# Expert chunks of a mixture of experts: ScalarE's Silu table load moved to the chunk's head, and the copy of the result shared with VectorE

## The chip, the cores and the metric

The kernel runs on one core of a Trainium2 chip, in one launch. The metric is the device time of that launch in microseconds (us). The kernel before has a median of 2042.09 us over 3 runs (2041.75 to 2046.13). About 0.2%, some 4 us, is what a measurement of this kernel can tell from no change.

## What is computed

Two layers with shared router weights. Each layer has modulated norms, a mixer (windowed attention beside a gated DeltaNet) and a grouped mixture of experts. The change lies in the experts alone. What they compute, cut from the reference:

```python
D_MODEL, D_FF, N_EXPERTS, DEPTH = 1024, 512, 16, 2      # 128 + 512 tokens, 2 experts each
xs = t[tok].astype(w_gate.dtype)                        # tokens sorted by expert
hid = jax.nn.silu(lax.ragged_dot(xs, w_gate, sizes)) * lax.ragged_dot(xs, w_up, sizes)
y = lax.ragged_dot(hid, w_down, sizes)
y = y * gate.reshape(-1)[order][:, None].astype(y.dtype)
return jnp.zeros((B * L, D), y.dtype).at[tok].add(y).reshape(B, L, D)
```

## The kernel before, in words

The function `expert_phase` runs once per layer. The tokens of an expert are taken in chunks of up to 128; an expert has at least one chunk, and 37 chunks run in the two layers. Only the last chunk of an expert prepares the weights of the next expert (`last and not final` in the code). So there are three kinds of step from a chunk to the next: last to last (24 of them with both ends inside the stretch looked at here), last to not-last (4) and not-last to last (4).

Products are made in three parts, because TensorE's operands are rounded: a weight piece of 128 x 2048 is split into `w_hi` (a rounded copy, ScalarE, `split` at L2061) and `w_lo` (what is left of it, a subtraction). There are six pieces per expert: 0 and 1 of the gate matrix, 2 and 3 of up, 4 and 5 of down. VectorE makes `w_lo` of pieces 0 to 4 (L2121), GpSimd that of piece 5 (L1952). The gathered tokens are turned by TensorE (L1973) and split in the same way into `x_hi` (ScalarE, L2058) and `x_lo` (VectorE, L2116), and so are the turned hidden values (L2096, L2148). The raw pieces of the next expert are loaded by SyncE's queue, each as soon as the `w_lo` before it in its place is made.

Every engine has its own hand-written order (`chunk(e, k, last, final)` in each of the five blocks), with semaphores between them:

- TensorE (L2018 to L2052): second half of the gate product, turn of the next chunk's tokens, the whole up product, then `gate_head`, the first half of the gate product of the next chunk, with the two turns of the hidden values in it, and last the down product into the PSUM banks 5 and 6 (L2043, L2044, L2049). `gate_head` waits for `x_lo` of the next chunk and for `w_lo` of piece 0.
- ScalarE (L2070 to L2105): `next_hi(0)`, a one-element Silu (L2081, tile `warm`) that brings in Silu's table, the Silu of the gate (L2084), `x_hi` and the pieces 1 to 4 in turn, then the copy of the finished result `y` out of PSUM (L2101, 128 x 1024), `next_hi(5)`, and the DMA of `y` to DRAM (L2105), which ScalarE's own queue issues after a wait for the copy. Behind this the queue runs the loop's branches and register loads, and the next chunk begins.
- VectorE (L2123 to L2152): `w_lo` of piece 0, the first half of `x_lo`, the two halves of `hid`, piece 1, the hidden low parts, the second half of `x_lo`, pieces 2, 3 and 4.
- GpSimd (L1949 to L1961): the gather of tokens two chunks ahead, and `w_lo` of piece 5.

Of the kernel before, what the change touches and what calls it, by code (L numbers as in the profile page):

```python
# [14 lines left out]
ACT = mybir.ActivationFunctionType  # L15
# [1843 lines left out]
def expert_phase(nc, l, A, G, R):  # L1859
# [11 lines left out]
    with ExitStack() as ctx:  # L1871
        ph = Phase(nc, ctx, "expert", l)
# [12 lines left out]
        y = ph.sb("y", [P, D])  # L1885
        cur = ph.sb("cur_idx", [P, 1], I32)
        warm = ph.sb("warm", [P, 1])
        raw_in = [ph.sem(f"raw_in{j}") for j in range(PIECES)]
        picked, g_half, g_p, u_half, u_p, xt_p, ht_p, d_half, y_p, w_hi_done, w_lo_done = (
            ph.sem(n) for n in "picked g_half g_p u_half u_p xt_p ht_p d_half y_p w_hi_done w_lo_done".split())  # L1890
        w_lo_last = ph.sem("w_lo_last")
        sg_done, hid_done, x_hi_done, x_lo_done, h_hi_done, h_lo_done, y_done, y_out, passed = (
            ph.sem(n) for n in "sg_done hid_done x_hi_done x_lo_done h_hi_done h_lo_done y_done y_out passed".split())
        gathered = ph.dma_sem(G.soft["gathered"])
# [9 lines left out]
        def hid_turned(m):  # L1904
            return G.ps[:, 4 + 3 * m, 0:HQ * P]
# [16 lines left out]
        with nc.Block() as block:  # L1922
# [45 lines left out]
            @block.tensor  # L1968
            def _(pe):
                def turn(k):  # L1970
                    pe.wait_ge(gathered, k * 16 + 16)
                    for n in range(KD):
                        tr = pe.transpose(turned[:, n * P:(n + 1) * P], xg[:, n:D:KD], G.c("ident"))  # L1973
                    tr.then_inc(xt_p, 1)

                def hid_turn(k, m):
                    pe.wait_ge(hid_done, k * 2 + (m + 2))
                    for n in range(HQ):
                        q = m * HQ + n
                        tr = pe.transpose(hid_turned(m)[:, n * P:(n + 1) * P], hid[:, q:FF:KF], G.c("ident"))  # L1980
                    tr.then_inc(ht_p, 1)

                def product(bank, q, j):

                    w, at = slice(q % 4 * FF, q % 4 * FF + 512), slice(q * P, (q + 1) * P)
                    pe.matmul(bank, x_hi[:, at], w_hi[:, j, w], start=(q == 0), stop=False)  # L1986
                    pe.matmul(bank, x_hi[:, at], w_lo[:, j, w], start=False, stop=False)  # L1987
                    return pe.matmul(bank, x_lo[:, at], w_hi[:, j, w], start=False, stop=(q == KD - 1))  # L1988

                def gate(q):  # L1990
                    return product(G.ps[:, 0, :], q, q // 4)

                def up(q):
                    return product(G.ps[:, 1, :], q, 2 + q // 4)

                def gate_head(e, k, between):

                    pe.wait_ge(x_lo_done, k * 2 + 1)
                    pe.wait_ge(w_lo_done, e * LP + 1)
                    for q in range(4):  # L2000
                        mm = gate(q)
                        if q in between:
                            between[q]()
                    mm.then_inc(g_half, 1)

                for s in (u_p, xt_p, ht_p, y_p):
                    pe.sem_inc(s, 1)
                turn(0)
                gate_head(0, 0, {})

                def chunk(e, k, last, final):
                    pe.wait_ge(x_lo_done, k * 2 + 2)
                    pe.wait_ge(w_lo_done, e * LP + 2)
                    for q in range(4, KD):
                        mm = gate(q)
                    mm.then_inc(g_p, 1)
                    if not (last and final):
                        turn(k + 1)  # L2018
                    pe.wait_ge(hid_done, k * 2 + 1)
                    for q in range(KD):  # L2020
                        if q % 4 == 0:
                            pe.wait_ge(w_lo_done, e * LP + (3 + q // 4))
                        mm = up(q)
                        if q % 4 == 3:
                            mm.then_inc((u_half, u_p)[q // 4], 1)
                    if last and final:
                        hid_turn(k, 0)
                        hid_turn(k, 1)
                    else:
                        pe.wait_ge(sg_done, k + 1)  # L2030
                        gate_head(e + 1 if last else e, k + 1, {1: lambda: hid_turn(k, 0), 2: lambda: hid_turn(k, 1)})
                    pe.wait_ge(y_done, k + 1)
                    for q in range(KF):
                        j, at = 4 + q // 2, slice(q * P, (q + 1) * P)
                        if q == 0:
                            pe.wait_ge(w_lo_done, e * LP + LP)
                        if q == 2:
                            pe.wait_ge(w_lo_last, e + 1)
                        if q % HQ == 0:
                            pe.wait_ge(h_hi_done, k * 2 + (q // HQ + 1))  # L2040
                        for h in range(2):
                            w = slice(q % 2 * D + h * 512, q % 2 * D + (h + 1) * 512)
                            pe.matmul(G.ps[:, 5 + h, :], h_hi[:, at], w_hi[:, j, w], start=(q == 0), stop=False)  # L2043
                            pe.matmul(G.ps[:, 5 + h, :], h_hi[:, at], w_lo[:, j, w], start=False, stop=False)  # L2044
                        if q % HQ == 0:
                            pe.wait_ge(h_lo_done, k * 2 + (q // HQ + 1))
                        for h in range(2):
                            w = slice(q % 2 * D + h * 512, q % 2 * D + (h + 1) * 512)
                            mm = pe.matmul(G.ps[:, 5 + h, :], h_lo[:, at], w_hi[:, j, w], start=False, stop=(q == KF - 1))  # L2049
                        if q % 2:  # L2050
                            mm.then_inc((d_half, y_p)[q // 2], 1)

                for_experts(pe, chunk)

            @block.scalar
            def _(act):
                def take(m):
                    act.activation(x_hi[:, x_half(m)], turned[:, x_half(m)], ACT.Copy).then_inc(x_hi_done, 1)  # L2058

                def split(j):  # L2060
                    act.activation(w_hi[:, j, :], raw[:, j, :], ACT.Copy).then_inc(w_hi_done, 1)  # L2061
# [10 lines left out]
                def chunk(e, k, last, final):  # L2072
                    def next_hi(j):

                        if last and not final:
                            act.wait_ge(raw_in[j], e * 16 + 16)
                            act.wait_ge((g_half, g_p, u_half, u_p, d_half, y_p)[j], k + (1, 1, 1, 2, 1, 2)[j])
                            split(j)

                    next_hi(0)  # L2080
                    act.activation(warm[:, :], G.eps[:, :], ACT.Silu)  # L2081
                    act.wait_ge(g_p, k + 1)
                    act.wait_ge(hid_done, k * 2 + 1)
                    act.activation(sg[:, :], G.ps[:, 0, :], ACT.Silu).then_inc(sg_done, 1)  # L2084
                    if not (last and final):
                        act.wait_ge(xt_p, k + 3)
                        act.wait_ge(u_half, k + 1)
                        take(0)
                    next_hi(1)
                    if not (last and final):  # L2090
                        act.wait_ge(u_p, k + 2)
                        take(1)
                    act.wait_ge(y_p, k + 1)
                    for m in range(2):
                        act.wait_ge(ht_p, k * 2 + (m + 2))
                        act.activation(h_hi[:, m * HQ * P:(m + 1) * HQ * P], hid_turned(m), ACT.Copy).then_inc(h_hi_done, 1)  # L2096
                        next_hi(2 + m)
                    next_hi(4)
                    act.wait_ge(y_p, k + 2)
                    act.wait_ge(y_out, k * 16 + 16)  # L2100
                    act.activation(y[:, :], G.ps[:, 5:7, :].rearrange("p b n -> p (b n)"), ACT.Copy).then_inc(y_done, 1)  # L2101
                    next_hi(5)
                    act.wait_ge(y_done, k + 2)
                    dst = A.y_table.rearrange("(c p) n -> c p n", p=P)[bass.ds(k, 1)].rearrange("a p n -> p (a n)")
                    act.dma_start(dst, y[:, :]).then_inc(y_out, 16)  # L2105

# [6 lines left out]
            def _(dve):  # L2113
# [6 lines left out]
                    dve.wait_ge(w_hi_done, e * PIECES + (j + 1))  # L2120
                    dve.tensor_tensor(w_lo[:, j, :], raw[:, j, :], w_hi[:, j, :].bitcast(F32), ALU.subtract).then_inc(w_lo_done, 1)  # L2121

                dve.sem_inc(hid_done, 1)  # L2123
                split(0, 0)
                for m in range(2):
                    take(0, m)
# [3 lines left out]
                def chunk(e, k, last, final):  # L2130
                    def next_lo(j):
                        if last and not final:
                            split(e + 1, j)
# [16 lines left out]
                            take(k + 1, 1)  # L2150
                    for j in range(2, LP):
                        next_lo(j)  # L2152

                for_experts(dve, chunk)
        ph.close()
# [164 lines left out]
```

## Time and profile before

| what | value |
|---|---|
| median of 3 runs | 2042.09 us |
| time of the profiled execution | 2047.7 us |
| its span, first to last instruction | 2045.9 us |
| TensorE busy (share of the span) | 1757.2 us (86%) |
| VectorE busy | 1219.8 us (60%) |
| ScalarE busy | 1022.2 us (50%) |
| GpSimd busy | 403.9 us (20%) |

The busy times are unions of the instructions' intervals on an engine. TensorE's (PE) are pipelined, so that 86% is not 86% of its peak. In the rows below DVE is VectorE, ACT is ScalarE, POOL is GpSimd, PEld is TensorE's weight load, and a q behind an engine's name is its queue (its sequencer), which waits, branches and issues DMAs. The expert phases lie at about 663 to 1040 us and 1650 to 2013 us of the span.

### The profile page before, as it was taken

The page shows a single profiled execution, that of the slowest core. Times are in us where ns is not written, and L with a number is a line of the kernel's source. Part 1 is how long each engine was busy: PE and PEld are TensorE (multiplying, and loading weights), DVE is VectorE, ACT ScalarE, POOL GpSimd, SP SyncE. Part 2 cuts the span into 40 slices and gives each one's busy share as a digit, 9 for nine tenths or more (in the row PEclk, how much of TensorE's full clock was granted, in tenths as well). Part 3 has the DMA queues.
Part 4 walks back from the last instruction along what each step waited for, and adds up shares of the span by engine and source line. Part 5 has one row for each costly group of instructions (what it writes and reads, how often), then busy time and mean ns, then how long its engine had stood idle before and what let it go on. Part 6 is the DMA issues. An engine that isn't in the chain of part 4 may idle for free. (4 is left out here: it accounts for less than half of the span.)

```text
span 2045.9 us, 39615 instructions
## 1 busy us (share of the span) xinstructions
PE 1757.2 (86%) x15349; PEld 1444.1 (71%) x15350; DVE 1219.8 (60%) x1815; ACT 1022.2 (50%) x1564; POOL 403.9 (20%) x293
## 2 busy tenths in 40 slices
PE   3998988999896899999949998899989959999992
PEld 0898677788653778778738886788875547777872
DVE  1388254566545875875554873556663477777563
ACT  2244522333422886886644454233332258888661
POOL 0000022212100342342230001212220024334221
PEclk7999998999897899999969999999998979999996
DMA  7221093331114898997563111342003279999854
GB/s 317 72 83 45 18 376 127 125 126 54 63 65 165 333 376 309 338 377 269 215 224 113 42 44 55 125 152 69 2 2 116 83 296 369 366 391 370 321 195 175
DMA packets 113580, 376.62 MB, mean 184 GB/s; under 512 B 15178, under 2 KB 35938, under 8 KB 87846
## 3 DMA queue, kind: packets, MB, share of 16 engines
q1 hardware_dynamic: 84782, 303.86, 40.3%
q10 hardware_dynamic: 20168, 39.89, 5.1%
q0 software_dynamic: 8496, 30.94, 4.1%
q8 instruction: 103, 1.69, 0.3%
q14 instruction: 31, 0.25, 0.0%
HBM read 332.87 MB, written 41.78 MB: 183 GB/s over the span
## 5 line engine op out<-in xcount | busy, mean ns | idle before, releaser
L2121 DVE TENSOR_TENSOR expert_w_lo<-shared,expert_w_hi 128x2048 fp32r<-128x2048 f32 x160 | 389.6, 2468 | 166.5 <-ACT expert_w_hi L2061 166.4
L2061 ACT ACTIVATE expert_w_hi<-shared 128x2048 fp32r<-128x2048 f32 x192 | 366.8, 1915 | 46.5 <-PEq L143 40.0
L1986 PE MATMUL ps<-expert_w_hi,expert_x_hi 128*128 128x512 f32 x592 | 245.8, 415 | 49.3 <-DVE expert_x_lo L2116 49.3
L1988 PE MATMUL ps<-expert_w_hi,expert_x_lo 128*128 128x512 f32 x592 | 233.8, 395 | 0.0
L1987 PE MATMUL ps<-expert_w_lo,expert_x_hi 128*128 128x512 f32 x592 | 233.7, 395 | 0.0
L1952 POOL TENSOR_TENSOR expert_w_lo<-shared,expert_w_hi 128x2048 fp32r<-128x2048 f32 x32 | 150.8, 4712 | 364.9 <-ACT expert_w_hi L2061 364.9
L1986 PEld LDWEIGHTS ps<-expert_w_hi,expert_x_hi 128*128 128x128 f32 x592 | 113.6, 192 | 81.2 <-DVE expert_w_lo L2121 51.2
L1127 POOL TENSOR_TENSOR mixer_NTb<-mixer_Bt,consts_sb 128x256 f32<-128x256 f32 x120 | 88.4, 760 | 283.3 <-DVE mixer_Bt L1402 220.1
L1988 PEld LDWEIGHTS ps<-expert_w_hi,expert_x_lo 128*128 128x128 f32 x592 | 112.6, 190 | 24.3
L1987 PEld LDWEIGHTS ps<-expert_w_lo,expert_x_hi 128*128 128x128 f32 x592 | 113.2, 191 | 18.7
L2043 PE MATMUL ps<-expert_w_hi,expert_hid_hi 128*128 128x512 f32 x296 | 115.8, 391 | 0.5 <-ACT expert_hid_hi L2096 0.5
L2044 PE MATMUL ps<-expert_w_lo,expert_hid_hi 128*128 128x512 f32 x296 | 115.3, 390 | 0.0
L1420 DVE TENSOR_TENSOR mixer_X<-mixer_X,ps 128x256 f32<-128x256 f32 x100 | 42.1, 421 | 109.1 <-PE ps L1216 107.2
L624 PE MATMUL ps<-projection_hT_hi,kvrows_r 128*128 128x256 f32 (+1 forms) x384 | 89.9, 315 | 9.6 <-DVE shared_r L531 9.6
L1339 ACT ACTIVATE mixer_T<-ps 128x256 f32<-128x256 f32 x100 | 38.4, 384 | 119.1 <-PE ps L1216 115.3
L2049 PE MATMUL ps<-expert_w_hi,expert_hid_lo 128*128 128x512 f32 x296 | 91.1, 389 | 0.0
L588 PE MATMUL ps<-shared_r,projection_hT_hi 128*128 128x512 f32 (+1 forms) x240 | 89.2, 372 | 0.0
L628 PE MATMUL ps<-projection_hT_hi,shared_r 128*128 128x256 f32 (+1 forms) x384 | 88.1, 311 | 0.0
L801 DVE SCALAR_TENSOR_TENSOR shared<-shared,projection_cwT 128x644 f32<-128x644 f32 x96 | 85.2, 888 | 2.5
L959 POOL MEMSET qkvT<- 128x512 f32 (+1 forms) x2 | 0.8, 418 | 393.6 <-POOLq L143 393.6
L624 PEld LDWEIGHTS ps<-projection_hT_hi,kvrows_r 128*128 128x128 f32 x384 | 70.0, 191 | 10.8 <-DVE shared_r L531 10.7
L1573 PE MATMUL ps<-shared,qkvT 128*128 128x512 f32 x160 | 76.0, 620 | 0.0
(372 smaller groups left out, 3856.5 us busy)
## 6 DMA issues: line engine op xcount, KB each, us to landing
shared<-in_w_up SPq DMA_DIRECT2D x64, 1024.0 KB, 7.5
shared<-in_w_down SPq DMA_DIRECT2D x64, 1024.0 KB, 8.1
shared<-in_w_gate SPq DMA_DIRECT2D x64, 1024.0 KB, 7.3
qkv<-in_w_ada SPq DMA_DIRECT2D x20, 1280.0 KB, 6.3
shared<-in_w_in SPq DMA_DIRECT2D x10, 2048.0 KB, 8.4
y_table<-expert_y ACTq DMA_DIRECT2D x37, 512.0 KB
qkvT<-in_w_ada SPq DMA_DIRECT2D x20, 768.0 KB, 8.6
y_table<-zero ACTq DMA_DIRECT2D x1, 12800.0 KB, 50.9
```

The lines of the kernel that those rows point to most:

```text
L588: pe.matmul(out, hi, w_lo, start=False, stop=False)
L624: pe.matmul(out, w_hi[:, k, :], h_hi[:, k, t * P:until * P], start=(k == 0), stop=False)
L1127: return pool.tensor_tensor(NTb[:, slot, d], Bt[:, d], row(G.c(f"level{level}_{d}"), DH), ALU.mult)
L1952: pool.tensor_tensor(w_lo[:, LP, :], raw[:, LP, :], w_hi[:, LP, :].bitcast(F32), ALU.subtract).then_inc(w_lo_last, 1)
L1986: pe.matmul(bank, x_hi[:, at], w_hi[:, j, w], start=(q == 0), stop=False)
L1987: pe.matmul(bank, x_hi[:, at], w_lo[:, j, w], start=False, stop=False)
L1988: return pe.matmul(bank, x_lo[:, at], w_hi[:, j, w], start=False, stop=(q == KD - 1))
L2043: pe.matmul(G.ps[:, 5 + h, :], h_hi[:, at], w_hi[:, j, w], start=(q == 0), stop=False)
L2044: pe.matmul(G.ps[:, 5 + h, :], h_hi[:, at], w_lo[:, j, w], start=False, stop=False)
L2049: mm = pe.matmul(G.ps[:, 5 + h, :], h_lo[:, at], w_hi[:, j, w], start=False, stop=(q == KF - 1))
L2061: act.activation(w_hi[:, j, :], raw[:, j, :], ACT.Copy).then_inc(w_hi_done, 1)
L2121: dve.tensor_tensor(w_lo[:, j, :], raw[:, j, :], w_hi[:, j, :].bitcast(F32), ALU.subtract).then_inc(w_lo_done, 1)
```

## The change

Three edits. ScalarE's one-element Silu moves from behind `next_hi(0)` to ahead of it. ScalarE copies only bank 5 of the result (128 x 512); bank 6 is copied by VectorE, at the end of its chunk, behind the `w_lo` of pieces 2 to 4. A new semaphore `y_low` says that VectorE's half is done; TensorE waits for it ahead of the next down product, and ScalarE ahead of the DMA of `y`.

```diff
-        w_lo_last = ph.sem("w_lo_last")
+        w_lo_last, y_low = ph.sem("w_lo_last"), ph.sem("y_low")
...
                     pe.wait_ge(y_done, k + 1)
+                    pe.wait_ge(y_low, k + 1)
                     for q in range(KF):
...
+                    act.activation(warm[:, :], G.eps[:, :], ACT.Silu)
                     next_hi(0)
-                    act.activation(warm[:, :], G.eps[:, :], ACT.Silu)
                     act.wait_ge(g_p, k + 1)
...
                     act.wait_ge(y_p, k + 2)
                     act.wait_ge(y_out, k * 16 + 16)
-                    act.activation(y[:, :], G.ps[:, 5:7, :].rearrange("p b n -> p (b n)"), ACT.Copy).then_inc(y_done, 1)
+                    act.activation(y[:, 0:512], G.ps[:, 5, :], ACT.Copy).then_inc(y_done, 1)
                     next_hi(5)
                     act.wait_ge(y_done, k + 2)
+                    act.wait_ge(y_low, k + 2)
                     dst = A.y_table.rearrange("(c p) n -> c p n", p=P)[bass.ds(k, 1)].rearrange("a p n -> p (a n)")
                     act.dma_start(dst, y[:, :]).then_inc(y_out, 16)
...
-                dve.sem_inc(hid_done, 1)
+                for s in (hid_done, y_low):
+                    dve.sem_inc(s, 1)
...
                     for j in range(2, LP):
                         next_lo(j)
+                    dve.wait_ge(y_p, k + 2)
+                    dve.wait_ge(y_out, k * 16 + 16)
+                    dve.tensor_copy(y[:, 512:1024], G.ps[:, 6, :]).then_inc(y_low, 1)
```

**The head of a chunk on ScalarE**, for the last chunk of an expert. Before:

```order
L2076 ISA
L2077 REGISTER_ALU
L2061 ACT_TABLE_LOAD
L2061 ACTIVATE expert_w_hi<-shared 128x2048
L2081 ACT_TABLE_LOAD
L2081 ACTIVATE expert_warm<-eps 128x1
L2083 ISA
L2084 ACTIVATE expert_sg<-ps 128x512
```

And in the changed kernel (line numbers from L2030 on are one higher, and more further down):

```order
L2081 ACT_TABLE_LOAD
L2081 ACTIVATE expert_warm<-eps 128x1
L2077 ISA
L2078 REGISTER_ALU
L2062 ACTIVATE expert_w_hi<-shared 128x2048
L2084 ISA
L2085 ACTIVATE expert_sg<-ps 128x512
```

One of the two table loads is gone: the copy of piece 0 (`w_hi`) needs none when Silu's table has been loaded ahead of it. The other now stands ahead of the register steps that wait for piece 0.

**The end of a chunk on VectorE**, where the copy of bank 6 comes in, in the changed kernel (before, the branch followed the third subtraction):

```order
L2123 TENSOR_TENSOR expert_w_lo<-shared,expert_w_hi 128x2048
L2122 REGISTER_ALU
L2123 TENSOR_TENSOR expert_w_lo<-shared,expert_w_hi 128x2048
L2157 ISA
L2158 COPY expert_y<-ps 128x512
L1918 REGISTER_ALU
L1918 COMPARE_AND_BRANCH
```

The last two rows are the loop's own steps: the copy is the last work of the chunk.

**The end of a chunk on ScalarE**, in the changed kernel; the shape of the copy and what ScalarE's queue waits for at L2107 are all that differs from before:

```order
L2102 ACTIVATE expert_y<-ps 128x512
L2062 ACTIVATE expert_w_hi<-shared 128x2048
L2107 ISA
L2107 DMA y_table<-expert_y 128x1024
L1918 REGISTER_ALU
L1918 COMPARE_AND_BRANCH
```

The branch and the register loads of the loop stand behind the DMA and its waits in the same queue.

## Rows read from the trace of the kernel before

**Rows 1.** The page: busy us, share of the span, instructions, by engine.
```profile
PE 1757.2 (86%) x15349; PEld 1444.1 (71%) x15350; DVE 1219.8 (60%) x1815; ACT 1022.2 (50%) x1564; POOL 403.9 (20%) x293
```
**Rows 2.** Busy time by stretch: PE, PEld, DVE, ACT, POOL, then clock, DMA share, GB/s.
```profile
695.77:1036.35 340.58, 320.65 (x1492) 263.65 (x1490) 216.31 (x177) 256.84 (x241) 111.02 (x49) 1.00 0.85 319
869.09:888.62 19.53, 18.08 (x86) 14.82 (x85) 14.88 (x12) 16.97 (x15) 7.80 (x3) 1.00 0.98 374
793.28:811.05 17.77, 17.77 (x86) 14.91 (x85) 5.16 (x8) 6.77 (x9) 5.72 (x3) 1.00 0.76 287
...
686.35:689.70 3.35, 3.35 (x11) 2.54 (x11) 2.54 (x3) 2.13 (x3) 0.00 (x0) 0.50 0.97 391
```
**Rows 3.** Waits by total: us, times, longest; 695:1036, then 1686:2010.
```profile
PE ps L1986 <- DVE expert_x_lo L2116: 18.9, 14, 1.5
...
PE ps L1986 <- DVE expert_x_lo L2116: 19.9, 14, 1.5
```
**Rows 4.** Timeline, ScalarE: start us, us, instruction, [idle before and what ended it].
```profile
869.09 1.03 ACT L2101 ACTIVATE expert_y<-ps 128x1024 f32<-128x1024 f32 x1 [0.81 <-PE ps L2049]
870.01 1.91 ACT L2061 ACTIVATE expert_w_hi<-shared 128x2048 fp32r<-128x2048 f32 x1
870.27 0.34 ACTq L2105 DMA_DIRECT2D y_table<-expert_y  x1
872.09 1.28 ACT L2061 ACT_TABLE_LOAD   x1 [0.17 <-issue]
873.38 1.92 ACT L2061 ACTIVATE expert_w_hi<-shared 128x2048 fp32r<-128x2048 f32 x1
875.32 1.28 ACT L2081 ACT_TABLE_LOAD   x1
876.62 0.20 ACT L2081 ACTIVATE expert_warm<-eps 128x1 f32<-128x1 f32 x1
876.72 0.58 ACT L2084 ACTIVATE expert_sg<-ps 128x512 f32<-128x512 f32 x1
877.20 0.59 ACT L2058 ACTIVATE expert_x_hi<-ps 128x512 fp32r<-128x512 f32 x1
```
**Rows 5.** Timeline, VectorE, the same step from chunk to chunk.
```profile
866.96 4.49 DVE L2121 TENSOR_TENSOR expert_w_lo<-shared,expert_w_hi 128x2048 fp32r<-128x2048 f32 x2
875.34 3.43 DVE L2121 TENSOR_TENSOR expert_w_lo<-shared,expert_w_hi 128x2048 fp32r<-128x2048 f32 x1 [3.89 <-ACT expert_w_hi L2061]
878.69 0.68 DVE L2116 TENSOR_TENSOR expert_x_lo<-ps,expert_x_hi 128x512 fp32r<-128x512 f32 x1
```
**Rows 6.** Timeline, GpSimd, the same step.
```profile
872.00 4.62 POOL L1952 TENSOR_TENSOR expert_w_lo<-shared,expert_w_hi 128x2048 fp32r<-128x2048 f32 x1 [10.90 <-ACT expert_w_hi L2061]
```
**Rows 7.** Timeline, TensorE: the first matmul of `gate_head` in this step.
```profile
879.52 0.49 PE L1986 MATMUL ps<-expert_w_hi,expert_x_hi 128*128 128x512 f32 x1 [1.45 <-DVE expert_x_lo L2116]
```
**Rows 8.** Timeline, ScalarE and TensorE, a step of the second layer.
```profile
1783.87 1.03 ACT L2101 ACTIVATE expert_y<-ps 128x1024 f32<-128x1024 f32 x1 [0.82 <-PE ps L2049]
...
1787.05 1.28 ACT L2061 ACT_TABLE_LOAD   x1 [0.35 <-issue]
...
1794.29 0.49 PE L1986 MATMUL ps<-expert_w_hi,expert_x_hi 128*128 128x512 f32 x1 [1.45 <-DVE expert_x_lo L2116]
```
**Rows 9.** Timeline, a step from a not-last to a last chunk: ScalarE, TensorE.
```profile
811.05 1.03 ACT L2101 ACTIVATE expert_y<-ps 128x1024 f32<-128x1024 f32 x1 [5.85 <-PE ps L2049]
...
814.45 1.28 ACT L2061 ACT_TABLE_LOAD   x1 [2.37 <-issue]
...
821.02 0.49 PE L1986 MATMUL ps<-expert_w_hi,expert_x_hi 128*128 128x512 f32 x1 [1.00 <-DVE expert_x_lo L2116]
```
**Rows 10.** Lines of the whole kernel, VectorE: another PSUM copy of that shape.
```profile
L926 DVE COPY kvrows<-ps 128x512 f32<-128x512 f32 x10 | 6.5, 687 | 6.2 <-PE ps L659 5.9
```
**Rows 11.** Timeline of the first chunk of layer one: TensorE, VectorE.
```profile
685.15 0.49 PE L1986 MATMUL ps<-expert_w_hi,expert_x_hi 128*128 128x512 f32 x1 [2.68 <-DVE expert_x_lo L2116]
...
690.40 6.88 DVE L2121 TENSOR_TENSOR expert_w_lo<-shared,expert_w_hi 128x2048 fp32r<-128x2048 f32 x3
```

## The prediction

> **What bounds the kernel now.** I read the page first, then busy time by stretch, then the waits, then the timeline of one step. The page [rows 1] shows TensorE at 86% and everything else far below, so time is lost or won where TensorE stands still. In the first expert phase it does so for 340.58 - 320.65 = 19.9 us [rows 2], and the waits name one cause for 18.9 us of it: the first matmul of `gate_head` waits for VectorE's `x_lo`, 14 times there and 14 times in the second layer [rows 3]. A last-to-last step takes 19.53 us with 18.08 us of TensorE [rows 2]; the 1.45 us between them is that wait [rows 7].
>
> So the question is what makes `x_lo` late. Count from Y, the start of ScalarE's result copy (869.09). ScalarE: copy to Y+1.03, high part of piece 5 to Y+2.83, table load at Y+3.00, high part of piece 0 from Y+4.29 to Y+6.21 [rows 4]. VectorE then subtracts piece 0 from Y+6.25 and needs 3.43 us, where the two subtractions before it took 4.49 us together, so about 2.28 each [rows 5]. The reader should see GpSimd beside it: its own subtraction runs from Y+2.91 to Y+7.53 [rows 6], and VectorE ends 2.15 us behind that, as if it had only begun when GpSimd ended. So TensorE is held by two things in turn: ScalarE's chain sets when VectorE may begin, GpSimd's instruction when it really does. `x_lo` follows at once (0.68 us), TensorE restarts at Y+10.43.
>
> **The Silu at the chunk's head.** Before, ScalarE loads a table, splits piece 0, loads Silu's table, and makes the one-element Silu (0.20 us) [rows 4]. Now the first load is Silu's and the second is gone, in 30 last chunks. ScalarE still has one load of 1.28 us ahead of piece 0, plus the small Silu, which delays it by 0.11 (876.62 to the next start at 876.72, and 0.01 of gap). What is saved, 1.28 us, lies behind piece 0, where in a last-to-last step nobody waits: `x_hi` ends at Y+8.70 and VectorE reaches `x_lo` only at Y+9.60 [rows 4, 5]. In the four not-last-to-last steps GpSimd is not in the way, and the path is ScalarE's: table load at Y+3.40, and TensorE idles 1.00 us [rows 9]. There `x_hi` is 1.28 us earlier, and VectorE's piece 0 is next. With the result copy 0.38 us shorter (below): load at Y+2.90, piece 0 from Y+4.30 to Y+6.22, VectorE to Y+8.54, `x_lo` to Y+9.14, TensorE at Y+9.29; it was at Y+9.97. That is 0.68 us for each, **-2.7 us** for four.
>
> A row against a rule: the load of 1.28 us starts 0.02 us behind the work before it and the next instruction starts 0.02 us behind it [rows 4]. The Trainium skill, ScalarE: Activation LUTs, What ACT_TABLE_LOAD costs, adds a drain of about 1.38 us to every switch; by it those four steps would win their whole 1.00 us, -4.0 us instead of -2.7. The trace shows no drain on this chip, so I keep the rows.
>
> **The result copy.** ScalarE's copy of 512 columns costs about what the Silu of that size does, 0.58 us [rows 4], so 0.45 less than 1.03. VectorE's half is priced by a copy of the same shape out of PSUM, 0.69 us [rows 10]. But VectorE comes to it only behind its third subtraction, which ends at 866.96 + 4.49 = 871.45, Y+2.36 [rows 5]. With the 0.08 us by which its instructions overlap, the copy runs from Y+2.28 to **Y+2.97**.
>
> **The new wait.** ScalarE's queue waits for that before it issues the DMA. Before, it had only its own copy to wait for (Y+1.03): DMA issue at 870.27, then the loop's branches and register loads, and the table load at 872.09, 1.97 us behind the copy's end. Those 1.97 us ran under the split of piece 5, which ended at Y+2.83; only 0.17 us showed as idle [rows 4]. That split was the cover, and it is gone: queued behind the wait are the DMA, the loop, the table load and piece 0. The order rows put the load ahead of two register steps; no row prices them, the bounds are 0 and the 0.17 us of idle, and I take 0.12 off, so 1.85 us. The load then starts at Y+4.82 and ends at Y+6.10, piece 0 runs from Y+6.22 to Y+8.13, VectorE's subtraction from Y+8.15. GpSimd, started 0.45 us earlier, has ended by Y+7.1 (by Y+7.6 if VectorE's copy held it off), so the subtraction takes its plain 2.28 us, to Y+10.43. `x_lo` overlaps it by 0.08 and ends at Y+11.03, TensorE restarts 0.15 later at **Y+11.18** instead of Y+10.43: +0.75 us. In the second layer the same branches take longer, 2.15 us from the copy's end to the load (1784.90 to 1787.05), for a restart at Y+10.42 [rows 8]; there it is Y+11.36, +0.94 us.
>
> Of the 24 steps, the first of each layer differs: VectorE ends at Y+1.51 there (690.40 + 6.88 against a Y of 695.77) [rows 11], so its copy ends at Y+2.12 and the step is about even in layer one, and some 0.5 us longer in layer two. The sum: 10 x 0.75 + 12 x 0.94 + 0.5 = **+19.3 us**.
>
> **Parts that cost nothing.** The four last-to-not-last steps have TensorE busy for all of 17.77 us [rows 2]; their Silu comes 2 us later, to about Y+6.9, and `x_lo` would be there at Y+8.1, against a TensorE free at Y+8.98; if that 0.9 us were used up they would pay too. TensorE's wait for `y_low` stands ahead of the next down product, far behind the copy, and the new copy's wait for the DMA of the chunk before (`y_out`) is for one issued a whole step earlier. VectorE's 0.69 us lie in its 3.89 us of idle [rows 5]. At the end of each layer the final result leaves 0.38 us earlier, **-0.8 us**.
>
> **The clock.** TensorE's gap grows from 1.45 to about 2.2 us in layer one and 2.4 in layer two. At 1.45 the granted clock stayed 1.00 (2.4 GHz) over the whole phase [rows 2]. After the gap of 2.68 us in the first chunk [rows 11] it read 0.50 (1.2 GHz) from 686.35 to 689.70 [rows 2]. The new gap lies between these two. What such a drop costs: from the restart to the next Y took 695.77 - 685.15 = 10.62 us there and 888.62 - 879.52 = 9.10 in a plain step, 1.52 us more on TensorE; but VectorE's third subtraction ended only 0.69 us later behind the restart (12.13 against 11.44), and VectorE is what the next step hangs on. So a drop costs 0.7 us, and the gap behind it is short again (about 1.35 us). The bounds are no drop at all and one after every second gap at the full 1.52, 0 to 18 us. The gap of 2.2 to 2.4 us is nearer to 2.68 than to 1.45, and none follows directly on a drop; I take a third of the gaps, 8 x 0.7 = **+5.6 us**.
>
> **Sum.** 19.3 - 2.7 - 0.8 + 5.6 = +21.4 us. Against the profiled execution's 2047.7 us that makes 2069.1. That execution lies 5.6 us above the median of the runs, so the median should be 2042.1 + 21.4 = **2063.5 us**.
>
> **Rivals.**
>
> *The shorter copy frees GpSimd, and it is faster.* By the rows GpSimd's subtraction is what VectorE really waits for; it begins when piece 5 is split, which is 0.45 us earlier now. If ScalarE's queue lost nothing at the new wait, each of the 24 steps would be 0.44 us shorter: -10.6 - 2.7 - 0.8 = -14 us, 2028 us. The Trainium skill, SBUF — State Buffer, Who interferes with whom, says that a VectorE instruction with two SBUF inputs and a GpSimd one that reads SBUF exclude each other whole; VectorE's end 2.15 us behind GpSimd's agrees, and by that rule alone this rival is the outcome. It decides if VectorE's copy is done by about Y+2.2, since the rest of the path takes 8.2 us; the rows put it at Y+2.97. A DMA share of 0.98 in a step [rows 2] speaks against it too: the weight loads leave little room for a shorter step, and a longer one relieves them. 8 in 100.
>
> *The two effects meet.* If the loop's steps cost less once nothing runs beside them, or the copy waits less, the restart stays within 0.15 us of now and the 24 steps add under 4 us: 2039 to 2046 us. Against it: it needs 0.6 us off a chain whose rows hardly vary. 6 in 100.
>
> *The clock falls after most gaps.* If VectorE falls behind as much as TensorE after each drop, and 14 gaps have one, it is 14 x 1.52 = 21 in place of 5.6: 2042.1 + 15.8 + 21 = 2079 us. For it, the distance to 2.68; against it, the first chunk's 0.69. 8 in 100.
>
> That the change would not do what it says is excluded for the table load: the order rows show it gone.
>
> **How the numbers follow.** The forecast has 78 in 100. Its own range goes from no drops and 1.8 us of loop in both layers (19.3 becomes 16; +12.5) to 8 more drops at full cost (+34). I give 2051 to 2077, which leaves out the faster and the even case and most of the third rival. A measurement can tell 0.2%, 4 us: faster 0.08, same 0.06, slower 0.86.
>
> **What would show it.** Right: ScalarE's table loads at L2061 gone (30 of them, 38 us of ScalarE), the one load per last chunk at about Y+4.8 with some 2 us of idle ahead of it instead of 0.17, VectorE's subtraction of piece 0 at 2.28 us, TensorE's gap at 2.2 to 2.4 us, and the step at 20.3 to 20.5 us. Wrong: a step under 19.5 us, VectorE's copy ending before Y+2.2, or the load starting earlier than 1.8 us behind VectorE's copy. The number of stretches at 1.2 GHz inside the expert phases settles the clock term.

## The result, and the profile after

The changed kernel takes 2066.18 us (median of 4 runs, 2064.75 to 2068.91) against 2043.69 us of the kernel before on the same chips (4 runs, 2041.75 to 2046.13). The ratio is 1.0111 with a 95% interval of 1.0093 to 1.0129: slower by 22.5 us, where 21.4 had been forecast. The profiled execution took 2064.75 us, with a span of 2063.0 us.

The page gives the busy times of the changed kernel, which answer to [rows 1]:

```profile
PE 1761.8 (85%) x15349; PEld 1445.9 (70%) x15350; DVE 1217.0 (59%) x1852; ACT 963.9 (47%) x1534; POOL 358.9 (17%) x293
```

Every helper engine works less than before, ScalarE by 58 us, and the kernel is slower. VectorE has 25.3 us of copies more and is still no busier, since its subtraction of piece 0 no longer lasts 3.43 us. GpSimd's 45 us less lie in its 37 index copies of 128x1 (L1944), which take 372 ns each instead of 1715. The groups of lines say what happened (count | busy us, mean ns of one | idle before, and what ended it):

```profile
L2081 ACT ACT_TABLE_LOAD x34 | 43.6, 1283 | 78.3 <-issue 78.2
L2158 DVE COPY expert_y<-ps 128x512 f32<-128x512 f32 x37 | 25.3, 684 | 37.4 <-PE ps L2050 37.4
L2102 ACT ACTIVATE expert_y<-ps 128x512 f32<-128x512 f32 x37 | 22.1, 598 | 65.2 <-PE ps L2050 65.2
```

The 30 table loads ahead of piece 0 are gone (38.5 us of ScalarE). The 34 that stay have 78.2 us of idle ahead of them that ended with "issue": ScalarE stood ready, and its queue had not yet come to the instruction.

A last-to-last step of layer one, Y = 875.05. ScalarE's timeline (compare [rows 4]):

```profile
875.05 0.60 ACT L2102 ACTIVATE expert_y<-ps 128x512 f32<-128x512 f32 x1 [0.82 <-PE ps L2050]
875.54 1.91 ACT L2062 ACTIVATE expert_w_hi<-shared 128x2048 fp32r<-128x2048 f32 x1
878.20 0.34 ACTq L2107 DMA_DIRECT2D y_table<-expert_y  x1
879.87 1.28 ACT L2081 ACT_TABLE_LOAD   x1 [2.41 <-issue]
881.16 0.20 ACT L2081 ACTIVATE expert_warm<-eps 128x1 f32<-128x1 f32 x1
881.27 1.90 ACT L2062 ACTIVATE expert_w_hi<-shared 128x2048 fp32r<-128x2048 f32 x1
883.08 0.57 ACT L2085 ACTIVATE expert_sg<-ps 128x512 f32<-128x512 f32 x1
```

VectorE's, GpSimd's and TensorE's in the same step (compare [rows 5 to 7]):

```profile
872.90 4.49 DVE L2123 TENSOR_TENSOR expert_w_lo<-shared,expert_w_hi 128x2048 fp32r<-128x2048 f32 x2
877.30 0.68 DVE L2158 COPY expert_y<-ps 128x512 f32<-128x512 f32 x1
883.21 2.29 DVE L2123 TENSOR_TENSOR expert_w_lo<-shared,expert_w_hi 128x2048 fp32r<-128x2048 f32 x1 [5.22 <-ACT expert_w_hi L2062]
...
877.54 4.61 POOL L1952 TENSOR_TENSOR expert_w_lo<-shared,expert_w_hi 128x2048 fp32r<-128x2048 f32 x1 [13.69 <-ACT expert_w_hi L2062]
...
886.25 0.49 PE L1986 MATMUL ps<-expert_w_hi,expert_x_hi 128*128 128x512 f32 x1 [2.22 <-DVE expert_x_lo L2118]
```

Read it as a chain. VectorE's copy ends at 877.98 (Y+2.93). ScalarE's queue issues the DMA at 878.20, not at Y+1.2 as before, and the table load follows at Y+4.82, after 2.41 us of idle that was 0.17. The split of piece 0 starts at Y+6.22, 1.93 us later than before, VectorE subtracts it in its plain 2.29 us because GpSimd ended at 882.15, and TensorE restarts at Y+11.20. In the second layer (compare [rows 8]) the load and the restart stand at Y+5.02 and Y+11.39, with Y = 1855.21:

```profile
1860.23 1.28 ACT L2081 ACT_TABLE_LOAD   x1 [2.61 <-issue]
...
1866.60 0.49 PE L1986 MATMUL ps<-expert_w_hi,expert_x_hi 128*128 128x512 f32 x1 [2.42 <-DVE expert_x_lo L2118]
```

Busy time by stretch (PE, PEld, DVE, ACT, POOL, then clock, DMA share, GB/s): that step, a not-last-to-last one (compare [rows 9]), a step with a stretch of low clock, the step behind it, and the stretch of low clock itself:

```profile
875.05:895.32 20.27, 18.05 (x86) 14.82 (x85) 14.29 (x13) 15.14 (x14) 5.72 (x3) 1.00 0.97 367
...
814.53:832.95 18.42, 18.04 (x86) 14.82 (x85) 12.05 (x11) 13.39 (x13) 1.15 (x2) 1.00 0.57 180
713.04:734.93 21.89, 19.64 (x86) 15.81 (x85) 14.88 (x14) 15.13 (x14) 5.73 (x3) 0.92 0.93 345
734.93:754.74 19.81, 18.05 (x86) 14.82 (x85) 13.84 (x12) 15.15 (x14) 7.56 (x3) 1.00 0.97 362
724.75:728.10 3.35, 3.35 (x11) 2.56 (x10) 2.62 (x4) 0.80 (x2) 0.00 (x0) 0.50 1.01 419
```

Five such stretches at 1.2 GHz lie in the two expert phases behind their first chunks; before there was none. Summed over all steps from one result copy to the next, the changed kernel is 24.9 us longer than before: +27.3 in the 24 last-to-last steps, -2.5 in the four not-last-to-last ones, 0.0 elsewhere. The two profiled spans differ by 17.1 us only; the rest, 7.7 us less, lies outside these steps, 2.3 us ahead of layer one's first result copy and 5.4 us between the layers. The first chunks take 32.3 us in both kernels, and the medians (22.5 us) are the better measure.

### The profile page after: what moved, and what is told of

It is laid out like the page before. It is cut to its first block and busy times, and to the rows that moved or that the text cites. A ratio compares the mean times of both kernels' runs of the same rounds, so it can differ in the third digit from the quotient of the medians.

```text
span 2063.0 us, 39735 instructions
## 1 busy us (share of the span) xinstructions
PE 1761.8 (85%) x15349; PEld 1445.9 (70%) x15350; DVE 1217.0 (59%) x1852; ACT 963.9 (47%) x1534; POOL 358.9 (17%) x293
## 5 line engine op out<-in xcount | busy, mean ns | idle before, releaser
L2123 DVE TENSOR_TENSOR expert_w_lo<-shared,expert_w_hi 128x2048 fp32r<-128x2048 f32 x160 | 365.6, 2318 | 168.8 <-ACT expert_w_hi L2062 168.8
L1988 PEld LDWEIGHTS ps<-expert_w_hi,expert_x_lo 128*128 128x128 f32 x592 | 114.0, 193 | 24.9
L2081 ACT ACT_TABLE_LOAD x34 | 43.6, 1283 | 78.3 <-issue 78.2
```

## The experiments

My theory was that the loss is all in what ScalarE's queue holds behind its wait for VectorE's half: loop, table load and piece 0. The rivals: the moved Silu costs; the shared copy itself costs; GpSimd's subtraction is still what binds. "Plain" below means a step without low clock.

**e1, the Silu alone.** The kernel before with one edit:

```diff
+                    act.activation(warm[:, :], G.eps[:, :], ACT.Silu)
                     next_hi(0)
-                    act.activation(warm[:, :], G.eps[:, :], ACT.Silu)
```

> Only the Silu moves to the chunk's head; ScalarE copies the whole result again and nothing waits for VectorE's half. My theory (the queue's wait for VectorE's copy makes the whole loss): last-to-last steps stay at 19.5 us with TensorE's gap at 1.45 us, because GpSimd's subtraction ends at Y+7.53 as before; the four not-last-to-last steps get some 0.3 us shorter (table load off the path of x_hi, then VectorE's piece 0 binds); in all -1 us against the kernel before. Rival (the moved Silu delays piece 0 and that is what costs): steps of 19.6 us and more, +2.6 us or more, and the half copy alone would then be cheap.

Measured: 2041.69 us, ratio 0.9988 (0.9980 to 0.9997), 2.2 us faster. All 24 last-to-last steps stay at 19.5 us with a gap of 1.45 us; the four others take 18.70 instead of 19.03 to 19.07. The Silu's move is no cost; its gain is small because in the common step GpSimd's instruction covers it.

**e2, the shared copy alone.** The changed kernel with the Silu back behind piece 0.

```diff
-                    act.activation(warm[:, :], G.eps[:, :], ACT.Silu)
                     next_hi(0)
+                    act.activation(warm[:, :], G.eps[:, :], ACT.Silu)
```

> Only the result copy is shared, the Silu stays behind piece 0. My theory: steps of 20.2 us in layer one and 20.5 in layer two as in the changed kernel (the load is now for Copy and starts about 1.9 us behind VectorE's copy), not-last-to-last steps 0.38 us shorter than before (18.67), in all +20 to +25 us against before. Rival (the Silu costs): within 3 us of before.

Measured: 2078.68 us, ratio 1.0162 (1.0142 to 1.0181), 35 us slower: more than I expected, and more than both edits together. Plain steps take 20.6 us in both layers. ScalarE, VectorE and TensorE in one of them (Y = 1889.12):

```profile
1894.10 1.28 ACT L2062 ACT_TABLE_LOAD   x1 [2.58 <-issue]
...
1897.33 1.28 ACT L2082 ACT_TABLE_LOAD   x1
...
1899.21 0.59 ACT L2059 ACTIVATE expert_x_hi<-ps 128x512 fp32r<-128x512 f32 x1
...
1897.34 2.29 DVE L2123 TENSOR_TENSOR expert_w_lo<-shared,expert_w_hi 128x2048 fp32r<-128x2048 f32 x1 [5.27 <-ACT expert_w_hi L2062]
1899.83 0.69 DVE L2118 TENSOR_TENSOR expert_x_lo<-ps,expert_x_hi 128x512 fp32r<-128x512 f32 x1 [0.19 <-ACT expert_x_hi L2059]
...
1900.66 0.49 PE L1986 MATMUL ps<-expert_w_hi,expert_x_hi 128*128 128x512 f32 x1 [2.57 <-DVE expert_x_lo L2118]
```

What I had missed: once GpSimd no longer holds VectorE off, VectorE is done with piece 0 before `x_hi` is there, and the second table load is on the path (the 0.19 us that end with ScalarE's `x_hi`). So beside the shared copy the Silu at the head is worth 0.3 us of each layer-one step, though beside GpSimd's subtraction it was worth nothing. The larger gap (2.58 us) also has ten stretches of low clock behind it instead of five.

**e3, VectorE's copy ahead of its last subtraction.** The changed kernel with its three lines moved up:

```diff
-                    for j in range(2, LP):
+                    for j in range(2, LP - 1):
                         next_lo(j)
                     dve.wait_ge(y_p, k + 2)
                     dve.wait_ge(y_out, k * 16 + 16)
                     dve.tensor_copy(y[:, 512:1024], G.ps[:, 6, :]).then_inc(y_low, 1)
+                    next_lo(LP - 1)
```

> The changed kernel, but VectorE copies its half ahead of the subtraction of piece 4 instead of behind it, so at about Y+0.1 to Y+0.8. My theory: the table load starts at about Y+2.5 behind piece 5; but the subtraction of piece 4 then runs from Y+0.75 to Y+3.0 and keeps GpSimd's subtraction, ready at Y+2.5, from starting until Y+3.0, so GpSimd ends at Y+7.6 and TensorE restarts at about Y+10.45: steps of 19.5 us, no 1.2 GHz stretches behind the first chunk, and with 18.4 us for the not-last-to-last steps -3 us against before. Rival (GpSimd and VectorE don't exclude each other, ScalarE's chain alone counts): restart at about Y+9.0, steps near 18.1 us, -30 us. Rival (GpSimd may start at once): steps of 19.1 us, -13 us.

Measured: 2037.21 us, ratio 0.9968 (0.9957 to 0.9980). The same work in another order is 29 us faster than the changed kernel and 6.6 us faster than the one before. Steps take 19.37 to 19.44 us, and no stretch of low clock lies behind a first chunk. VectorE and GpSimd (Y = 865.07):

```profile
865.14 0.68 DVE L2158 COPY expert_y<-ps 128x512 f32<-128x512 f32 x1
865.75 2.28 DVE L2123 TENSOR_TENSOR expert_w_lo<-shared,expert_w_hi 128x2048 fp32r<-128x2048 f32 x1
871.05 3.62 DVE L2123 TENSOR_TENSOR expert_w_lo<-shared,expert_w_hi 128x2048 fp32r<-128x2048 f32 x1 [3.02 <-ACT expert_w_hi L2062]
...
867.56 4.96 POOL L1952 TENSOR_TENSOR expert_w_lo<-shared,expert_w_hi 128x2048 fp32r<-128x2048 f32 x1 [10.48 <-ACT expert_w_hi L2062]
```

GpSimd was ready at 867.56 but needed 4.96 us instead of 4.62, as VectorE's subtraction ran to 868.03; it ended at 872.52, and VectorE's piece 0, begun at 871.05, ended 2.15 us behind that. The early copy took the wait away, and the old bound came back: the 0.45 us that ScalarE wins shrink to 0.1.

**e4, piece 5 on VectorE, with the kernel before's copy.** e1, and the subtraction of piece 5 moved from GpSimd to the end of VectorE's chunk:

```diff
                         gather(nc.s_assert_within(k + 2, 2, MAXC))
-                        if last:
-                            split_last(e + 1)
...
                     for j in range(2, LP):
                         next_lo(j)
+                    if last and not final:
+                        split_last(e + 1)
```

> e1, and in addition the low part of piece 5 is made by VectorE at its chunk's end instead of by GpSimd. VectorE is idle from Y+2.36 to Y+6.25 and the subtraction needs 2.28 us there once piece 5 is split at Y+2.83. My theory (GpSimd's instruction is what binds the kernel before, by keeping VectorE off): VectorE takes piece 0 at Y+6.3 for 2.28 us, TensorE's gap falls from 1.45 to about 0.4 us, steps of 18.5 us, -24 us against before. Rival (the weight loads bind, DMA share 0.98 in a step): ScalarE waits for raw pieces and steps stay at 19.1 to 19.5 us, -10 to 0 us. Rival (VectorE becomes the bound): steps over 19.5 us, slower.

Measured: 2007.00 us, ratio 0.9823 (0.9806 to 0.9841), 37 us faster, of which 2 are e1's and 35 this move's. VectorE's timeline and the stretch of the step (Y = 855.00):

```profile
857.86 2.29 DVE L2118 TENSOR_TENSOR expert_w_lo<-shared,expert_w_hi 128x2048 fp32r<-128x2048 f32 x1 [0.51 <-ACT expert_w_hi L2054]
861.19 2.29 DVE L2114 TENSOR_TENSOR expert_w_lo<-shared,expert_w_hi 128x2048 fp32r<-128x2048 f32 x1 [1.03 <-ACT expert_w_hi L2054]
...
855.04:873.35 18.31, 18.05 (x86) 14.83 (x85) 16.11 (x13) 15.68 (x15) 2.41 (x2) 1.00 1.02 420
```

VectorE's piece 0 begins where it did before (Y+6.2) and takes 2.29 us instead of 3.43; steps fall to 18.3 (18.5 in layer two) from 19.5. The steps account for 26.7 us, 1.3 of them e1's. A further 7.5 us come from the first chunks, where TensorE waited in the same way (28.5 us to the first result copy instead of 32.3). The weight loads kept up, at 420 GB/s instead of 374.

**e5, ScalarE's queue freed.** The changed kernel, with the DMA of `y` and its two waits in GpSimd's queue, behind its subtraction, and a small first DMA in that queue ahead of the first gather:

```diff
-                    act.wait_ge(y_done, k + 2)
-                    act.wait_ge(y_low, k + 2)
-                    act.dma_start(dst, y[:, :]).then_inc(y_out, 16)
...
+                    pool.wait_ge(y_done, k + 2)
+                    pool.wait_ge(y_low, k + 2)
+                    pool.dma_start(dst, y[:, :]).then_inc(y_out, 16)
```

> The changed kernel, but the DMA of the result and its two waits stand in GpSimd's queue, behind its subtraction of piece 5, instead of in ScalarE's; VectorE's copy stays at the end of its chunk. My theory (the loss is what queues behind the wait on ScalarE): the table load follows piece 5 at about Y+2.5, GpSimd binds again (from Y+2.5 to Y+7.1, which holds VectorE off until then), TensorE restarts at about Y+10.0: steps of 19.1 us, no 1.2 GHz stretch behind the first chunk, -13 us against before. Rival (VectorE's copy itself, or TensorE's new wait, costs): steps stay over 20 us, +20 us.

Measured: 2034.22 us, ratio 0.9954 (0.9935 to 0.9972), 9.5 us faster. VectorE's copy stays as late as in the changed kernel, and it no longer matters. ScalarE, VectorE and GpSimd (Y = 865.79), the step, and a result copy of ScalarE in layer two:

```profile
868.21 1.28 ACT L2086 ACT_TABLE_LOAD   x1
...
868.06 0.68 DVE L2159 COPY expert_y<-ps 128x512 f32<-128x512 f32 x1
871.54 3.50 DVE L2124 TENSOR_TENSOR expert_w_lo<-shared,expert_w_hi 128x2048 fp32r<-128x2048 f32 x1 [2.80 <-ACT expert_w_hi L2068]
...
868.27 4.62 POOL L1953 TENSOR_TENSOR expert_w_lo<-shared,expert_w_hi 128x2048 fp32r<-128x2048 f32 x1 [10.46 <-ACT expert_w_hi L2068]
...
865.77:884.85 19.08, 18.05 (x86) 14.82 (x85) 15.53 (x13) 15.37 (x14) 7.81 (x4) 1.00 0.99 380
...
1758.36 0.60 ACT L2107 ACTIVATE expert_y<-ps 128x512 f32<-128x512 f32 x1 [2.22 <-DMA y_table<-expert_y]
```

This is the rival of the prediction, alive as soon as its condition holds: GpSimd starts 0.43 us earlier than before, VectorE ends 2.15 us behind it, and the step is 0.43 us shorter. I had expected 13 us in all. The steps give 11.3, although one DMA of `y`, issued at 1744.92, landed late and held up ScalarE's copy at 1758.36: that step took 20.5 us, and the next one, with a stretch of 1.2 GHz, 20.7. The first chunks are 3.3 and 3.6 us longer. The first DMA of the new queue is the likely cause: in e10, where it stands behind the first gather, they are 1.3 us longer than in e4 and e7.

**e6, VectorE copies twice.** The changed kernel with the same copy into a spare tile ahead of its own.

```diff
+                    dve.tensor_copy(sg2[:, :], G.ps[:, 6, :])
                     dve.tensor_copy(y[:, 512:1024], G.ps[:, 6, :]).then_inc(y_low, 1)
```

> The changed kernel with VectorE copying the bank twice, the first time into a spare tile: y_low comes 0.6 us later. My theory (each us of y_low's lateness is a us of every last-to-last step): steps of 20.9 us in layer one and 21.1 in layer two, gaps of 2.85 to 3.05 us, 1.2 GHz behind most of the gaps, so at least +14 us against the changed kernel (+36 us against before) and with the clock up to +30 (+52). Rival (VectorE's and ScalarE's spare time cover it): no change against the changed kernel.

Measured: 2101.72 us, ratio 1.0280 (1.0260 to 1.0300): 58 us over the kernel before, 36 over the changed one. The two plain steps of layer one take 20.84 and 20.91 us, 0.6 more for 0.6 us of copy. Most gaps, of 2.0 to 3.3 us, have a stretch of low clock behind them, so the total is over my upper figure.

**e7, the late copy with piece 5 on VectorE.** The changed kernel with e4's second edit.

> The changed kernel with the low part of piece 5 on VectorE, behind its late copy. My theory (in the changed kernel the wait alone sets the step, GpSimd has dropped out): steps stay at 20.3 and 20.5 us, +14 to +24 us against before, although the same move took 1.0 to 1.2 us off every step in e4. Rival (GpSimd still binds): steps of 19.1 to 19.3 us.

Measured: 2061.24 us, ratio 1.0090 (1.0071 to 1.0108). Its plain step:

```profile
751.87:772.16 20.29, 18.04 (x86) 14.82 (x85) 16.52 (x14) 15.13 (x14) 2.42 (x2) 1.00 0.97 359
```

The step is the changed kernel's, 20.29 us. Freeing VectorE of GpSimd, worth 1.2 us a step in e4, is worth nothing behind the wait. The 5 us under the changed kernel come from the first chunks, 28.5 us to the first result copy instead of 32.3 in both layers (7.6 us); the steps take 2.4 us more in sum, with six stretches of low clock instead of five.

**e8, all three that help.** e3 with e4's second edit: Silu at the head, copy ahead of piece 4, piece 5 on VectorE.

> e3 with the low part of piece 5 on VectorE: Silu at the head, VectorE's copy ahead of piece 4, no subtraction on GpSimd. My theory: ScalarE's load at Y+2.65 (2.85 in layer two), VectorE's piece 0 from Y+5.98 (6.17), TensorE's gap 0.05 (0.25) us, steps of 18.1 (18.3) us, 18.4 for the not-last-to-last ones: -6 us against e4, -42 against before. Rival (weight loads bind under 18.3 us a step): no faster than e4. Rival (VectorE late with pieces 4 and 5, busy without a break from Y+0.1 to Y+5.3): piece 0 starts late or TensorE waits in the down product, slower than e4.

Measured: 2003.00 us, ratio 0.9799 (0.9783 to 0.9815). Steps of a layer each:

```profile
837.26:855.42 18.16, 18.05 (x86) 14.82 (x85) 16.66 (x14) 15.29 (x14) 2.42 (x2) 1.00 1.00 392
1730.80:1749.09 18.29, 18.06 (x86) 14.83 (x85) 16.61 (x14) 15.26 (x14) 2.42 (x2) 1.00 1.00 403
```

That is within 0.06 us of the forecast; against e4 the steps' sum is 6.0 us less and the medians differ by 4.0.

**e9, the wait without the shared copy.** ScalarE copies the whole result; VectorE only clears one element per partition at its end.

```diff
-                    act.activation(y[:, 0:512], G.ps[:, 5, :], ACT.Copy).then_inc(y_done, 1)
+                    act.activation(y[:, :], G.ps[:, 5:7, :].rearrange("p b n -> p (b n)"), ACT.Copy).then_inc(y_done, 1)
...
-                    dve.tensor_copy(y[:, 512:1024], G.ps[:, 6, :]).then_inc(y_low, 1)
+                    dve.memset(mark[:, :], 0.0).then_inc(y_low, 1)
```

> The changed kernel with the wait but without the shared copy: ScalarE copies the whole result again, and VectorE only clears one element per partition at the end of its chunk, which y_low then tells of. My theory (the place of the wait costs, the copy behind it only adds its own 0.6 us): y_low comes at about Y+2.4 to Y+2.5, the table load at Y+4.3 in layer one and Y+4.5 in layer two, steps of 19.7 and 19.9 us, so +7 us against before in the 24 steps, and -1 us for the others: about +6. Rival (sharing the copy costs, not the wait): like e1, no slower than before.

Measured: 2056.74 us, ratio 1.0072 (1.0053 to 1.0091), 12.6 us slower where I expected 6. The load stands at Y+4.26 and plain steps take 19.71 us in layer one and 19.91 and 19.95 in layer two (the others there have low clock or follow a step that has it), as forecast. ScalarE (Y = 867.93), and two steps of layer two:

```profile
870.52 0.34 ACTq L2108 DMA_DIRECT2D y_table<-expert_y  x1
872.19 1.28 ACT L2082 ACT_TABLE_LOAD   x1 [1.43 <-issue]
...
1700.02:1721.63 21.61, 19.60 (x86) 15.78 (x85) 14.44 (x14) 15.56 (x15) 7.38 (x3) 0.92 0.95 361
...
1721.63:1741.12 19.49, 18.04 (x86) 14.83 (x85) 13.32 (x12) 15.55 (x15) 7.80 (x3) 1.00 0.96 359
```

The rest is the clock: six steps of layer two have a stretch of 1.2 GHz behind a gap of only 1.86 to 2.01 us. In layer one, with gaps of 1.65 to 1.75 us, there is none.

**e10, the freed queue with piece 5 on VectorE.** e5 with e4's second edit, and the first DMA of the queue behind the first gather.

> e5 with the low part of piece 5 on VectorE (behind its late copy), and the small first DMA of the new queue behind the first gather. My theory: ScalarE's load at Y+2.42 in both layers, VectorE's piece 0 from Y+5.76, TensorE never idle: steps of 18.05 us, 17.76 for the not-last-to-last ones, -5 to -7 us against e8, so about 1997 us. Rival (result DMAs from GpSimd's queue share the DMA engines with the weight loads and land late, as one step of 20.5 us in e5 hints): single long steps, no faster than e8.

Measured: 1997.38 us, ratio 0.9781 (0.9760 to 0.9803), 47 us faster than before and the fastest of all:

```profile
854.50:872.38 17.88, 17.88 (x86) 14.83 (x85) 16.61 (x14) 15.38 (x15) 3.21 (x3) 1.00 1.00 406
```

TensorE is busy without a gap, in steps of 17.85 to 17.91 us (the first of each layer takes 18.05 and 18.06). No step with a late DMA showed here.

| kernel | Silu first | copy of bank 6 | waits for it | piece 5 | plain step, layer 1 / 2 | ratio |
|---|---|---|---|---|---|---|
| before | no | ScalarE | - | GpSimd | 19.5 / 19.5 | 1 |
| e1 | yes | ScalarE | - | GpSimd | 19.5 / 19.5 | 0.9988 |
| e2 | no | VectorE, late | ScalarE | GpSimd | 20.6 / 20.6 | 1.0162 |
| changed | yes | VectorE, late | ScalarE | GpSimd | 20.3 / 20.5 | 1.0111 |
| e7 | yes | VectorE, late | ScalarE | VectorE | 20.3 / 20.5 | 1.0090 |
| e6 | yes | VectorE, late, twice | ScalarE | GpSimd | 20.9 / - | 1.0280 |
| e9 | yes | ScalarE | ScalarE, for a mark | GpSimd | 19.7 / 19.9 | 1.0072 |
| e3 | yes | VectorE, early | ScalarE | GpSimd | 19.4 / 19.4 | 0.9968 |
| e5 | yes | VectorE, late | GpSimd | GpSimd | 19.1 / 19.1 | 0.9954 |
| e4 | yes | ScalarE | - | VectorE | 18.3 / 18.5 | 0.9823 |
| e8 | yes | VectorE, early | ScalarE | VectorE | 18.2 / 18.3 | 0.9799 |
| e10 | yes | VectorE, late | GpSimd | VectorE | 17.9 / 17.9 | 0.9781 |

## Why the prediction was right, point by point

**What bounds the kernel: right.** That TensorE waits for VectorE, which waits for GpSimd's instruction, is shown by e4: VectorE starts piece 0 at the same place, GpSimd's subtraction is gone, and the gap falls from 1.45 to 0.26 us in layer one and to 0.45 to 0.60 in layer two. e3 and e5 show the same 2.15 us from GpSimd's end to VectorE's, wherever GpSimd starts.

**The new wait: right, and the whole cause, with the low clock that follows the longer gaps.** Restart at Y+11.18 and Y+11.36 forecast, Y+11.20 and Y+11.39 measured. The plain steps of layer one cost 0.76 us each (0.75 forecast), those of layer two 0.99 on average (0.94 forecast), and with the first of each layer they come to 19.9 us where the sum said 19.3. e5 shows that it is the queue: with the waits elsewhere the late copy costs nothing. e6 shows the slope, e7 that GpSimd has no part in it, and e9 splits it: the place of the wait alone is worth 0.2 and 0.4 us a step, the copy behind it the other 0.55.

**The Silu at the head: right in this kernel, incomplete as a rule.** -2.7 us was forecast for the four not-last-to-last steps, -2.5 measured, and restarts at Y+9.35 (forecast Y+9.29). That is 0.62 us each, not the 1.00 that the prediction reckoned if there were a drain; nor would that follow from its own path, on which VectorE's piece 0 comes next. "In a last-to-last step nobody waits" was read from the rows of before, where GpSimd still held VectorE off. It fails as soon as that is gone: e2 against the changed kernel shows the second load on the path. The changed kernel was spared this only since both edits came together. No drain behind a table load shows in any run, as in the rows of before: all but four loads of each run have the next instruction 0.01 us behind them.

**The clock: the count and the size were both off, in opposite directions.** The term said 8 x 0.7 = 5.6 us. There were five stretches of low clock, and such a step took 1.5 to 1.6 us more, of which the next step gave back 0.5 once and next to nothing otherwise: 27.3 - 19.9 = 7.4 us. The step of the working that failed is the 0.7 us, taken from one first chunk, and with it the short gap of 1.35 us behind a drop: behind the five it was 1.76 us once and 2.14 to 2.42 three times, and one was followed by a last-to-not-last step, which has no gap to shorten.

In that first chunk the low clock began 1.17 us behind TensorE's restart (686.32 against 685.15). In the changed kernel it began between 0.28 us ahead of the restart and 0.80 us behind it, and the traces show that this place sets the price. The changed kernel, e2, e6, e7 and e9 have 47 such stretches behind a gap ahead of `gate_head`. In the 14 that begin 1.05 us or more behind the restart, VectorE's third subtraction ends at Y+1.5 of the next step, as behind the first chunk, and so the copy behind it comes early. In 10 of the 12 that begin at least 0.1 us ahead of the restart it ends at Y+2.3, as in a plain step; the other two, both in e6, are twice as long. Between these places the end moves steadily from 2.3 to 1.6. Two steps of e2 in a row, the first with low clock from 1.5 us behind the restart, and the stretch of low clock:

```profile
1763.59:1785.79 22.20, 19.62 (x86) 15.94 (x85) 15.43 (x14) 16.53 (x15) 5.72 (x3) 0.92 0.94 353
1785.79:1805.57 19.78, 18.06 (x86) 14.83 (x85) 13.64 (x12) 16.55 (x16) 7.24 (x3) 1.00 0.97 339
1776.66:1780.04 3.38, 3.38 (x12) 2.69 (x11) 2.95 (x4) 2.77 (x4) 0.00 (x0) 0.50 1.05 402
```

Against 20.62 us for a plain step of e2 the first pays 1.58 and the second gives back 0.84, which leaves the prediction's 0.7 us. So 0.7 is right for a drop that begins late and half of what it costs when it begins with the restart. That VectorE then waits for TensorE's slow turns of the hidden values is the likely reason, and not tested. The number of gaps was a choice between two rows, not a finding.

**The ends of the layers: not borne out in layer two, open in layer one.** -0.8 us was forecast for two earlier final results. In both layers the DMA of the last result is issued 0.25 us earlier behind Y. In layer two the first gather of the results follows 0.26 us earlier (Y+5.48 instead of Y+5.74), but the first instruction that needs it starts at Y+12.1 in both traces, and the stretch from the last result copy to the end of the span is 35.8 us in both. In layer one the first gather starts 1.0 us earlier (Y+6.27 instead of Y+7.26); how much of that is the change's was not tested.

**The sum: right, in part by luck.** The measured terms add up to 19.9 - 2.5 + 7.4 = +24.8 us in the traces, 3.4 above the forecast's 21.4. That the medians differ by 22.5 us, 1.1 from the forecast, owes something to the clock term's two opposite errors and to time outside the steps; the interval of the ratio is about 19 to 26 us.

**Rivals.** The shorter copy frees GpSimd: it did not happen, and e5 shows that it would have, with the restart where the rival put it. The clock falling after most gaps: not in the changed kernel; in e6, at 2.0 to 3.3 us.

## What to carry to other kernels

A wait in an engine's queue is paid by everything behind it in that queue: here a DMA issue whose own lateness cost nothing held up the loop's branches, a table load and the next split, 1.9 to 2.1 us of the queue's own steps that had run under another instruction. Before moving work to an idle engine, look where in that engine's order it becomes ready, and give the wait to a queue with nothing urgent behind it (e5), or put the work ahead of what need not be first (e3). And ask of two idle-looking helpers whether they exclude each other: GpSimd at 20% and VectorE at 60% busy were the bound, and moving one subtraction from the idler to the busier one (4.6 us there, 2.3 here) was worth 35 us.

## What the runs showed of the hardware that I had not expected

- **Low clock after gaps under 2 us.** Counted over the twelve traces, in the expert phases behind the first chunks: of 124 TensorE gaps of 1.0 to 1.79 us ahead of `gate_head` none had a granted clock of 0.50 with it; of 96 gaps of 1.85 to 3.4 us, 47 did, beginning within the gap or up to 1.5 us behind it. The shortest of these was 1.86 us. Gaps of equal size went both ways (the changed kernel: 2.25 us with, 2.24 us without; 2.45 us with, 2.42 us seven times without), so the size alone does not decide it. What does was not tested.
- **A DMA share of 0.98 left room.** The kernel before moved 374 GB/s in a step at a share of 0.98; e4 moved 420 and e10 406 at 1.02 and 1.00, without ScalarE waiting for a raw piece. Over all steps of layer one it was 319 GB/s at 0.85 before, 335 at 0.86 in e4 and 348 at 0.87 in e10. The share alone did not say that the loads were at their limit.
- **GpSimd and VectorE excluded each other in both directions.** VectorE's subtraction ended 2.15 us behind GpSimd's wherever it began (e3, e5), and GpSimd's took 4.96 instead of 4.62 us where VectorE's was running at its start (e3). GpSimd's index copy took 2.24 us beside VectorE's piece 0 in the kernel before (from 876.57) and 0.18 with VectorE idle in the changed one (from 882.10). VectorE's copy out of PSUM did not: GpSimd kept its 4.61 us beside it in the changed kernel. The Trainium skill, SBUF — State Buffer, Who interferes with whom, says this of a VectorE instruction with two SBUF inputs against a GpSimd one that reads SBUF, and says that one with at most one SBUF input does not contend outside the two-port modes. These rows agree; the copy out of PSUM has no SBUF input.
